# Cached pages laid four rows to a partition, and scores that read the turned keys in permuted order

## The reference, cut to what matters

```
def stick_breaking_weights(z, mask):
    log_keep = jnp.where(mask, jax.nn.log_sigmoid(-z), 0.0)
    remain = lax.cumsum(log_keep, axis=z.ndim - 1, reverse=True)
    return jnp.exp(jnp.where(mask, z + remain, -jnp.inf))

def sb_decode(q, k_new, v_new, k_past, v_past, bias):
    z_past = jnp.einsum('bqhd,bkhd->bhqk', q, k_past).astype(jnp.float32)
    z_new = jnp.einsum('bqhd,bkhd->bhqk', q, k_new).astype(jnp.float32)
    z = jnp.concatenate([z_past, z_new], axis=-1) * scale + bias[None, :, None, None]
    a = stick_breaking_weights(z, mask).astype(v_new.dtype)
    return (jnp.einsum('bhqk,bkhd->bqhd', a[..., :P], v_past)
            + jnp.einsum('bhqk,bkhd->bqhd', a[..., P:], v_new))

    k_past = cache_k[l][page_table].reshape(Bd, n_pages * PAGE_SIZE, SB_HEADS, SB_HEAD_DIM)
    v_past = cache_v[l][page_table].reshape(Bd, n_pages * PAGE_SIZE, SB_HEADS, SB_HEAD_DIM)
```

## Time and profile before

| what | us |
|---|---|
| median of 3 runs | 1584.86 |
| profiled execution | 1580.1 |
| its span, first to last instruction | 1578.4 |
| of this, page stage | 368 to 752 |
| TensorE busy in the span | 1362.0 |
| VectorE busy | 390.8 |
| ScalarE busy | 353.0 |

### The profile page before, as it was taken

How to read it: one execution, slowest core, us unless ns; L and a number is a source line. 1 busy time by engine, 2 the same in 40 slices (tenths; PEclk the granted TensorE clock), 3 DMA queues, 4 the chain that set the end, 5 groups by cost and what they waited for, 6 DMA issues and landing times.

```text
span 1578.4 us, 22203 instructions
## 1 busy us (share of the span) xinstructions
PE 1362.0 (86%) x8780; PEld 811.7 (51%) x8780; DVE 390.8 (25%) x691; ACT 353.0 (22%) x566; POOL 87.3 (6%) x144
## 2 busy tenths in 40 slices
PE   7999988986999999887699997978988888788873
PEld 5847444464676767554578884553333333233321
DVE  2013333333444444442010012241101010101113
ACT  2122233232544544664000001110100000000000
POOL 3000000002000000200000000010111001100100
PEclk9999999997999999999799998978998898889987
DMA  6113200005999999999680116036999999999984
GB/s 217 54 56 121 80 0 0 0 0 153 327 372 343 361 370 313 386 385 368 224 308 24 54 54 221 27 147 260 428 425 426 426 426 427 425 426 426 423 369 180
DMA packets 119640, 395.94 MB, mean 251 GB/s; under 512 B 17075, under 2 KB 25284, under 8 KB 107250
## 3 DMA queue, kind: packets, MB, share of 16 engines
q1 hardware_dynamic: 109506, 380.41, 62.1%
q0 software_dynamic: 5984, 11.18, 2.0%
q10 hardware_dynamic: 4048, 2.93, 0.6%
HBM read 386.06 MB, written 16.27 MB: 255 GB/s over the span
## 4 chain that ended last, share of the span: by engine, by line
PE 73%; issue 7%; DVE 6%; DMA 5%; SPq 4%; ACT 4%; ACTq 1%; POOLq 0%; DVEq 0%
PE ps L1091 16%; PE ps L932 8%; PE ps L1114 7%; PE ps L629 7%; PE ps L755 6%; PE ps L632 4%; PE ps L935 4%; PE ps L990 3%; PE ps L766 3%; DMA arena<-in_cache_k 3%; SPq L356 2%; PE ps L788 2%; PE ps L684 2%; SPq L348 1%; PE ps L688 1%
## 5 line engine op out<-in xcount | busy, mean ns | idle before, releaser
L1091 PE MATMUL ps<-arena 128*64 128x512 f32 x512 | 260.1, 667 | 73.5 <-issue 72.0
L1092 PE MATMUL ps<-arena 128*64 128x512 f32 x512 | 260.5, 669 | 0.0
L1091 PEld LDWEIGHTS ps<-arena 128*64 128x64 f32 x512 | 75.7, 154 | 222.5 <-issue 220.3
L755 PE MATMUL ps<-ident,arena 128*128 128x128 f32 x1024 | 149.3, 292 | 25.8 <-DMA arena<-in_cache_k 20.0
L755 PEld LDWEIGHTS ps<-ident,arena 128*128 128x128 f32 x1024 | 117.8, 148 | 96.2 <-issue 67.8
L1308 ACT ACTIVATE arena<-ps 128x512 f32<-128x512 f32 x192 | 108.7, 595 | 170.2 <-PE ps L755 170.0
L629 PE MATMUL ps<-mixers,arena 128*128 128x272 f32 x512 | 121.2, 399 | 0.5 <-DVE mixers L1460 0.5
L932 PE MATMUL ps<-mixers,arena 128*128 128x272 f32 x512 | 120.1, 396 | 0.0
L629 PEld LDWEIGHTS ps<-mixers,arena 128*128 128x128 f32 x512 | 98.5, 193 | 21.2 <-DVE mixers L1460 0.6
L932 PEld LDWEIGHTS ps<-mixers,arena 128*128 128x128 f32 x512 | 98.3, 192 | 20.5 <-issue 0.4
L632 PE MATMUL ps<-arena,mixers 128*128 128x512 f32 (+1 forms) x240 | 105.4, 595 | 0.0
(11 more groups left out here) (319 smaller groups left out, 1376.3 us busy)
## 6 DMA issues: line engine op xcount, KB each, us to landing
arena<-in_cache_k SPq DMA_DIRECT2D x256, 256.0 KB, 5.1
arena<-in_cache_v SPq DMA_DIRECT2D x256, 256.0 KB, 5.0
arena<-in_w_gate_exp SPq DMA_DIRECT2D x32, 2048.0 KB, 27.8
arena<-in_w_up_exp SPq DMA_DIRECT2D x32, 2048.0 KB, 32.2
arena<-in_w_down_exp SPq DMA_DIRECT2D x22, 2048.0 KB, 23.6
mixers<-in_w_down_exp SPq DMA_DIRECT2D x10, 2048.0 KB, 23.2
arena<-in_w_in SPq DMA_DIRECT2D x7, 2048.0 KB, 8.9
arena<-in_w_in SPq DMA_DIRECT2D x8, 1024.0 KB, 8.3
```

Source lines behind the costliest of these rows:

```text
L755: last = turn(ps[:, TURN + j % 2, P * c:P * c + P], kring[n % 3][:, j, P * c:P * c + P], ident[:, :])
L1091: mm(ps[0:BLK, 1 + u, :], own, wgv[w][:, k, :], start=k == 0, stop=k == KD - 1)
L1092: last = mm(ps[BLK:P, 1 + u, :], own, wuv[w][:, k, :], start=k == 0, stop=k == KD - 1)
```

## The change

A page's 128 rows are taken as 32 groups of four. Each group of four rows (8 KB, contiguous in memory) goes to one partition, and page j of the unit takes the partitions j, j + 4, j + 8 and so on. A page is still one transfer of 256 KB. Block r of a buffer (512 floats on each partition) now holds row 4 i + r of page g at partition 4 i + g, where before block j held page j.

Transposing is as before, block by block, so a turned key now stands at column 128 r + 4 i + g. `unit_scores` reads the turned keys with a pattern that brings them back to the logical order (128 g + 4 i + r): from one moving column to the next the address steps 128 floats (512 bytes) three times, and then back to the next i, 4 floats (16 bytes) on. The scores, their sum and all that VectorE does are in logical order as before. `set_weights` writes its 512 exponentials in the permuted order, with the same pattern on its output, so that block r of the turned weights fits block r of the values. No instruction is added, removed or moved on any engine; what changes is the shape of the page transfers on SyncE, of the 512 score matmuls' moving operand, and of 16 exponentials on ScalarE.

```
@@ key_loads
-                    sp.dma_start(kring[n % 3][:, j, :], a["cache_k"][0, bass.ds(page, 1)].rearrange("a s h d -> (a s) (h d)")
+                    sp.dma_start(flat(kring[n % 3])[j::GP, :],
+                                 a["cache_k"][0, bass.ds(page, 1)].rearrange("a (p r) h d -> (a p) (r h d)", r=GP)
                                  ).then_inc(S(f"cache_k_{n % 3}"), 16)
@@ value_loads
-                    sp.dma_start(vring[:, n % 3, j, :], a["cache_v"][0, bass.ds(page, 1)].rearrange("a s h d -> (a s) (h d)")
+                    sp.dma_start(flat(vring[:, n % 3])[j::GP, :],
+                                 a["cache_v"][0, bass.ds(page, 1)].rearrange("a (p r) h d -> (a p) (r h d)", r=GP)
                                  ).then_inc(S(f"cache_v_{n % 3}"), 16)
@@ unit_scores
-                    last = mm(ps[32 * c:32 * c + 32, ZB, :], qblk_of(m // NGRP, s, c), d_kt[:, n % 2, c, :],
+                    last = mm(ps[32 * c:32 * c + 32, ZB, :], qblk_of(m // NGRP, s, c),
+                              d_kt[:, n % 2, c, :].rearrange("p (r i g) -> p g i r", r=GP, g=GP),
                               start=s == 0, stop=s == PER_SET - 1)
@@ set_weights
-                fn(d_e, d_z, ACT.Exp).then_inc(S("set_weights"), 1)
+                fn(d_e.rearrange("p (r i g) -> p g i r", r=GP, g=GP), d_z.rearrange("p (g i r) -> p g i r", g=GP, r=GP),
+                   ACT.Exp).then_inc(S("set_weights"), 1)
```

## The result

The changed kernel takes 1620.2 us at the median of three of its four executions (1614.9 to 1627.0), against 1584.8 before; the ratio is 1.0235, 95% interval 1.0195 to 1.0274. The fourth, at 2682.8 us, stands apart and is left out. The forecast was 1574 us, faster; the range given (1562 to 1725) holds the time, but the sign was wrong.

The account below looks back on a forecast made before the run. TensorE was taken to set the pace before 640 us and the transfers after it. Transfers -14, the scores' strided read +3 and the exponential 0 summed to -11, so 1584.9 became 1574 us; range 1562 to 1725.

Parts of the forecast that it names:

- What bounds the kernel: Page stage: TensorE sets the pace before 640 us (5.77 us a unit), the transfers after it (5.41 us a unit).
- I take +0.07: Score matmuls' strided read: 1.00 to 1.07 us a unit, within bounds 0 and +2.85; +3 us over 46 units.
- the 16-byte line: Score reads: the Trainium skill's rule that crossing lines costs; at half rate 1.00 becomes 2.00 us a unit, 1620 in all.
- +3 - 4: Before 640 us: +3 for the scores' strided read (with the first 3 later units), -4 for faster landing of pages.
- SyncE's issue cost does not follow the row count ... so the floor stays: SyncE's page issues: cost per transfer unchanged, so the issue floor stays 4.78 us a unit, below the 5.41 us period.
- the 4.92 that I took for the transfers: Units after 640 us: 8 KB pieces at 426 GB/s need 4.92 us instead of 5.41, 9 us gained over 18 units.
- The transfers' -14: Page transfers in 8 KB pieces: -9 after 640 us, -4 before it, -1 at the end.
- The exponential: 16 ScalarE exponentials writing with jumps: between nothing and double (+0.63 us each), taken as 0; uncovered 10 us.
- A part of it: Rival on the scores' read: part of the shared-path slowdown, +0.42 or +0.93 us a unit, 1590 or 1617; chance 0.19.
- its second form: Scores: two accesses served at a time, 1.93 us a unit (+0.93), 18 other units at 5.09 us; +33, 1617.
- The shared path: Rival: the scores' four streams share one access path, +2.85 or +2.44 us a unit, 1735 or 1709; chance 0.27.
- next to nothing: Scores' strided read: one measured stream of spaced weight loads hardly slowed; the forecast resting on it (1562 to 1584) had 0.46.

Follow-up runs that it names:

- e10_pool2k: Kernel before with 2 KB pieces kept, only the value pages issued from GpSimd's queue instead of SyncE's; ratio 0.9973.
- e4_probe: Kernel before plus unread 512-column probe matmuls and two ScalarE copies after the last unit's scores; one strip 0.42 us a pass neighbouring, 0.91 permuted.
- e1_scores: Kernel before with only the score matmuls reading in the permuted order, transfers and exponentials unchanged; ratio 1.0186, about +29 us.
- e9_pool: Changed kernel with score order mended at ScalarE's PSUM read and value pages issued from GpSimd; 1561.0 us against 1580.7 for the kernel before, ratio 0.9880.
- e2_loads: Kernel before with only the page transfers changed to 8 KB pieces on every fourth partition; ratio 1.0147, +23 us.
- e5_adjacent: Kernel before with only the page transfers changed to 8 KB pieces, page j on 32 neighbouring partitions from 32 j on; ratio 1.1168.

## Why the prediction was wrong

- **What bounds the kernel** held: TensorE before 640 us, transfers after it. e10_pool2k bears out that SyncE's issue was not the bound: with half of the issues taken off it the ratio is 0.9973.
- **The step that failed first: "I take +0.07".** The scores' strided read costs +0.94 us a unit at 2.4 GHz. I judged it by the nearest row, the spaced weight loads, whose stream hardly slowed. A weight load and a moving operand are different reads: e4_probe shows the second at half rate already with one stream. The lengthening of the single load (193 against 141 ns) was the sign that I set aside, and the reading of the 16-byte line that I put beside it, half the rate, gave 2.00 us for the scores: the timeline has 1.94. Its effect is +29 where the sum had +3 - 4: the table has +29.0 up to the 45th unit, +28.5 in e1_scores alone.
- **The step that failed second: "SyncE's issue cost does not follow the row count ... so the floor stays".** The premise was right and the conclusion not: not the number of partitions but the step between them costs, 472 against 333 ns. (The 430 ns of the sample rows, which I quoted for it, showed already that an issue can cost more than 333 ns for some reason that I hadn't named; it is open still.) The floor went from 4.78 to 5.9 us a unit, over the 4.92 that I took for the transfers, so the 18 units after 640 us cost (5.9 - 5.41) x 18 = +9 instead of -9; the table has +7.9. With the +29 that is +37 to +38; the profiled spans differ by 34.7, the ratio says +37. No row of before had a partition step, and I should have given the issue bounds of its own as I did the read.
- **The transfers' -14** was right in size and not in effect: -15 once the floor is gone (e9_pool against e10_pool2k), +23 with it (e2_loads). Against the kernel before, e9_pool gains 3.2 us up to the 45th unit and 9.7 behind it, where the forecast had 4 and 9.
- **The exponential** doubled as at the upper bound (0.63 to 1.14), and is nearly hidden, at most 5 us by its interval.
- **The rivals.** "A part of it" came out: its second form, +0.93 a unit and 1617, has the right number by a wrong mechanism (two accesses at a time over four streams; in fact each stream by itself). Its rate for the 18 other units, 5.09, was missed through the issue floor, 5.94. The same holds for the 16-byte line at half the rate: it has the mechanism of the scores, and its 1620 us is the measured time, but by luck. It counted +46 where +29 came, and a gain in the last units where the floor took 8 us. The shared path, to which I gave more, is refuted by e4_probe. That I put the strided read at 0.46 for "next to nothing" was the error of judgement: one row of another operand against a written rule.

## What to carry to other kernels

In the shapes measured here a moving operand in float32 may skip one float and not three (two was not run): keep two neighbouring columns in 16 bytes, or put the permutation where it is read from PSUM by ScalarE, which cost nothing, and where it runs once for a set and not once for each unit. When a transfer's shape changes, its issue cost is a number of its own: hold the issues of a unit, each with the distance to the next one (0.66 us here for an issue of 0.47), against the period before counting on the rate, and avoid a step between partitions or share the issues between queues. A change with two prices and one gain may be worth keeping in part: here the transfers with both prices taken off gained 1.2%, about 0.3% of it by the second queue alone.

## What the runs showed of the hardware that I had not expected

- Spaced moving columns: 1088 to 1118 ns at the median instead of 592 for a 512-column pass, for steps of 16, 128 and 512 bytes, and at 512 bytes for one to four strips; a step of 8 bytes 618 ns.
- The same length at both clocks: the 512 score passes of the kernel after last 1071 to 1103 ns. A unit's scores at 609.41 us, where the granted clock was 0.50, take 1.96 us to the next transposes, at 2.4 GHz 1.94; neighbouring ones took 1.87 at the low clock and 1.00 at the high one. So spaced reads cost about what the low clock costs, and don't come on top of it. The timeline and the stretch of the kernel after:

```profile
609.41 2.03 PE L768 MATMUL ps<-arena 128*32 128x512 f32 x8
611.37 1.72 PE L757 MATMUL ps<-ident,arena 128*128 128x128 f32 x8
```

```profile
609.41:611.44 2.03, 2.03 (x10) 0.27 (x10) 1.57 (x2) 0.73 (x2) 0.00 (x0) 0.50 0.97 371
```

- ScalarE pays for jumps in SBUF and not in PSUM: a copy that writes with jumps 1142 ns, one that reads with them 1104 ns (neighbouring: 624 ns for the exponential of the same size), the read out of PSUM 682 ns as before. The two copies stand once each in e4_probe:

```profile
L1390 ACT ACTIVATE arena<-arena x1: 1142/1142/1142, 830.0 to 830.0; 128x512 f32<-128x512 f32 x1
L1391 ACT ACTIVATE arena<-arena x1: 1104/1104/1104, 830.9 to 830.9; 128x512 f32<-128x512 f32 x1
```

- Transfers into 32 neighbouring partitions: 250 GB/s at a full share (e5_adjacent, 392 to 640 us); into 32 on every fourth partition, after 640 us: 353 with a dear issue, 403 without it as the bound.
- The step between partitions made SyncE's issue dearer (472 against 333 ns) and not GpSimd's (526 against 546).
